# Retention in a two-block transformer kernel: a slab piece moved behind a head's outputs, ScalarE's copies moved ahead of SiLU, and one sum over added squares

## What is computed

```
def retention(q, k, v, g, positions):      # 4 heads; q, k: 128 wide, v, g: 256 wide
    q = rotary(q); k = rotary(k) * 128 ** -0.5
    scores = einsum('bnihd,bnjhd->bnhij', qc, kc) * decay_intra      # chunks of 128 tokens
    intra  = einsum('bnhij,bnjhe->bnihe', scores, vc)
    kv     = einsum('bnjhd,hj,bnjhe->nbhde', kc, decay_k, vc)
    _, prev = lax.scan(lambda state, kv_n: (decay_chunk * state + kv_n, state), 0, kv)
    cross  = einsum('bnihd,hi,nbhde->bnihe', qc, decay_q, prev)
    o = rms_norm(intra + cross)            # over the 256 features of one head
    return silu(g) * o                     # g = h @ w_in[:, 2048:3072]
```

## Time and profile before

| | us |
|---|---|
| median of 3 runs | 2892.36 |
| lowest and highest | 2891.91, 2897.39 |
| the profiled execution | 2891.22 |
| its span, first to last instruction | 2889.3 |
| TensorE busy | 2722.6 (94%) |
| VectorE busy | 1534.1 (53%) |
| ScalarE busy | 1106.3 (38%) |
| GpSimd busy | 906.2 (31%) |
| TensorE's granted clock, mean | 0.96 of full speed |

### The profile page before, as it was taken

The page is one execution under the profiler, slowest core; times in us unless marked ns, Lnnn a source line. Parts: engine busy times, 40 slices in busy tenths (PEclk is TensorE's granted clock), DMA queues, the critical chain, the costliest instruction groups (busy, mean ns, idle before and its releaser), DMA issues.

```text
span 2889.3 us, 34424 instructions
## 1 busy us (share of the span) xinstructions
PE 2722.6 (94%) x13278; PEld 2257.0 (78%) x13278; DVE 1534.1 (53%) x1676; ACT 1106.3 (38%) x1275; POOL 906.2 (31%) x200
## 2 busy tenths in 40 slices
PE   7899878999989999997989999899999979899997
PEld 5687567888769888886868888697988868788886
DVE  6755577699872420343256766754113351566666
ACT  3433353677642433334332233324432343332222
POOL 3211001000033244343434444242343433344343
PEclk9999698899999999998999999899999999999999
DMA  6110037499722122222234444221222222244443
GB/s 233 59 45 23 30 117 269 151 369 367 277 70 88 59 98 100 88 99 83 102 117 183 164 162 159 100 91 70 82 102 88 90 92 102 95 172 169 167 154 130
DMA packets 65320, 376.66 MB, mean 130 GB/s; under 512 B 7728, under 2 KB 8752, under 8 KB 29872
## 3 DMA queue, kind: packets, MB, share of 16 engines
q1 hardware_dynamic: 63040, 368.58, 35.1%
q10 hardware_dynamic: 2160, 6.42, 0.6%
HBM read 372.86 MB, written 2.10 MB: 130 GB/s over the span
## 4 chain that ended last, share of the span: by engine, by line
PE 75%; DVE 4%; issue 3%; POOL 1%; ACT 1%; ACTq 0%; DVEq 0%; POOLq 0%
PE pd L240 18%; PE pd L241 18%; PE pd L242 18%; PE pd L261 2%; PE pd L260 2%; PE pd L259 2%; PE pd L1768 2%; PE pd L1766 2%; PE pd L1767 2%; POOL sb_w_lo L218 1%; PE pd L1793 1%; DVE sb_ada_held L369 1%; PE pd L1795 1%; PE pd L1794 1%; PE pd L1724 1%
## 5 line engine op out<-in xcount | busy, mean ns | idle before, releaser
L218 POOL TENSOR_TENSOR sb_w_lo<-sb_raw,sb_w_hi 128x2048 fp32r<-128x2048 f32 x189 | 892.4, 4722 | 1792.7 <-ACT sb_w_hi L209 1792.7
L240 PE MATMUL pd<-sb_h_hi,sb_w_hi 128*128 128x512 f32 x1696 | 677.0, 399 | 44.0 <-DVE sb_h_lo L337 25.6
L241 PE MATMUL pd<-sb_h_lo,sb_w_hi 128*128 128x512 f32 x1696 | 666.7, 393 | 0.0
L242 PE MATMUL pd<-sb_h_hi,sb_w_lo 128*128 128x512 f32 x1696 | 666.0, 393 | 0.0
L209 ACT CAST sb_w_hi<-sb_raw 128x2048 fp32r<-128x2048 f32 x189 | 360.9, 1910 | 319.1 <-PE pd L242 315.0
L240 PEld LDWEIGHTS pd<-sb_h_hi,sb_w_hi 128*128 128x128 f32 x1696 | 322.8, 190 | 123.0 <-DVE sb_h_lo L337 29.7
L240 PE MATMUL pd<-sb_y_hi,sb_w_hi 128*128 128x512 f32 x960 | 377.2, 393 | 20.9 <-issue 17.0
L241 PE MATMUL pd<-sb_y_lo,sb_w_hi 128*128 128x512 f32 x960 | 376.4, 392 | 0.0
L242 PE MATMUL pd<-sb_y_hi,sb_w_lo 128*128 128x512 f32 x960 | 376.1, 392 | 0.0
L241 PEld LDWEIGHTS pd<-sb_h_lo,sb_w_hi 128*128 128x128 f32 x1696 | 322.8, 190 | 67.9 <-issue 2.2
L242 PEld LDWEIGHTS pd<-sb_h_hi,sb_w_lo 128*128 128x128 f32 x1696 | 322.3, 190 | 68.4
(11 more groups left out here) (502 smaller groups left out, 3918.1 us busy)
## 6 DMA issues: line engine op xcount, KB each, us to landing
sb_raw<-in_slabs SPq DMA_DIRECT2D x189, 1024.0 KB, 4.9
sb_V<-in_ada SPq DMA_DIRECT2D x64, 512.0 KB, 6.1
sb_V<-in_moe SPq DMA_DIRECT2D x28, 1024.0 KB, 7.1
sb_QK<-in_moe SPq DMA_DIRECT2D x28, 1024.0 KB, 7.1
sb_raw<-in_moe SPq DMA_DIRECT2D x28, 1024.0 KB, 6.8
sb_ada_held<-in_ada SPq DMA_DIRECT2D x36, 512.0 KB, 4.6
sb_QK<-in_ada SPq DMA_DIRECT2D x32, 512.0 KB, 6.7
sb_M<-in_ada SPq DMA_DIRECT2D x12, 512.0 KB, 14.3
```

The lines of the kernel that those rows point to most:

```text
L218: pool.tensor_tensor(w_lo[j][:], raw[j][:], w_hi[j][:].bitcast(F32), ALU.subtract).then_inc(w_lo_ready[j], 1)
L240: pe.matmul(out, w_hi[j][:, cols], hi[:, k], start=(k == 0), stop=False)
L241: pe.matmul(out, w_hi[j][:, cols], lo[:, k], start=False, stop=False)
L242: last = pe.matmul(out, w_lo[j][:, cols], hi[:, k], start=False, stop=(k == KT - 1))
```

## The change

Four things change, all in the retention loops.

- TensorE: `head_norm(h - 1)` moves from ahead of the gate slab to behind its third piece. The state products follow five pieces, not six. Of the remaining three pieces two stand ahead of the outputs, and the last one behind them.
- ScalarE: the wait for `ret_out` and the two copies stand ahead of SiLU instead of behind it. The squares stay behind SiLU.
- VectorE: `head_norm` begins with the sum of the two tiles of squares, behind both `ret_sq` signals, and signals `ret_added`.
- TensorE: `head_norm` has one matmul over that sum instead of two over the squares.

```diff
 # tensor engine
                 def head_norm(h):
-                    for et in range(2):
-                        pe.wait_ge(ret_sq, 8 * l + 2 * h + et + 1)
-                        last = pe.matmul(px[2][:], ones[:], T[:, et], start=(et == 0), stop=(et == 1))
-                    last.then_inc(ret_sum, 1)
+                    pe.wait_ge(ret_added, 4 * l + h + 1)
+                    pe.matmul(px[2][:], ones[:], T[:, 0], start=True, stop=True).then_inc(ret_sum, 1)
...
                     last.then_inc(ret_sc, 1)
+                    slab_starts(pe, L + L_G + h // 2, h % 2)
+                    for piece in range(3):
+                        slab_piece(pe, h % 2, piece, h_hi, h_lo)
                     if h:
                         head_norm(h - 1)
-                    slab_starts(pe, L + L_G + h // 2, h % 2)
-                    for piece in range(6):
+                    for piece in range(3, 5):
                         slab_piece(pe, h % 2, piece, h_hi, h_lo)
...
-                    for piece in range(6, KT):
+                    for piece in range(5, 7):
                         slab_piece(pe, h % 2, piece, h_hi, h_lo)
                     pe.wait_ge(ret_state, 4 * l + h + 1)
...
                     last.then_inc(ret_out, 1)
+                    slab_piece(pe, h % 2, KT - 1, h_hi, h_lo)
 # scalar engine
                     if h:
                         head_norm(h - 1)
+                    act.wait_ge(ret_out, 4 * l + h + 1)
+                    for et in range(2):
+                        act.copy(O[:, 2 * h + et], px[et][:]).then_inc(ret_stored, 1)
                     act.wait_ge(slab_done[j], m + 1)
                     act.wait_ge(ret_scaled, 4 * l + h + 1)
                     for f in range(2):
                         ins = act.activation(QK[:, 4 * f + h], pd[2 * j + f][:], ACT.Silu)
                     ins.then_inc(slab_out[j], 1)
-                    act.wait_ge(ret_out, 4 * l + h + 1)
-                    for et in range(2):
-                        act.copy(O[:, 2 * h + et], px[et][:]).then_inc(ret_stored, 1)
 # vector engine
                 def head_norm(h):

+                    dve.wait_ge(ret_sq, 8 * l + 2 * h + 2)
+                    dve.tensor_tensor(T[:, 0], T[:, 0], T[:, 1], ALU.add).then_inc(ret_added, 1)
                     dve.wait_ge(ret_root, 4 * l + h + 1)
```

More of the change, by code:

```diff
@@ L1518, in build @@
             "swapped", "rotated", "ret_sc", "ret_scaled", "ret_kv", "ret_state", "ret_out", "ret_stored"))
-        ret_sq, ret_sum, ret_root = (sem(n) for n in ("ret_sq", "ret_sum", "ret_root"))
+        ret_sq, ret_added, ret_sum, ret_root = (sem(n) for n in ("ret_sq", "ret_added", "ret_sum", "ret_root"))
         sgu_loaded, vs_root, vs_norm, sgu_w, mixed, mixed_out = (sem(n) for n in (
```

## The result

| | before | changed |
|---|---|---|
| median, us | 2896.12 | 2900.45 |
| lowest and highest, 11 runs each | 2891.78, 2900.58 | 2899.29, 2908.68 |
| ratio to before, 95% interval | | 1.0021 (1.0011 to 1.0031) |
| profiled execution: span, mean clock | 2889.3, 0.960 | 2901.9, 0.957 |

The change makes the kernel slower by 0.21%, 6 us (3 to 9 by the interval). Forecast were +11.9 us, twice as much; 2900.45 lies inside the range of 2894.5 to 2908. The kernel before had a median of 2896.12 in these runs, 3.7 us above the 2892.4 from which the forecast was counted, so the difference says more than the absolute time.

The account below looks back on a forecast made before the run. VectorE's serial chain, with 1.14 us to spare, was taken to become the bound through a later root; 3.6 us for waits plus 5 x 1.65 for clock falls gave +11.9, so 2892.4 + 11.9 = 2904.3 us, range 2894.5 to 2908.

Parts of the forecast that it names:

- VectorE's chain has 1.1 to 1.7 us to spare, and the change uses up 2.4 to 2.5: Retention heads: the root starts 2.4 to 2.5 us later, more than VectorE's serial chain to the state sums can spare.
- held about equally by both ways: Root's start at 7.7 us behind the outputs' end, set alike by ScalarE's order and by the sum's place on TensorE.
- The new wait of some 2.9 us: TensorE ahead of the outputs: there at 14.3, it waits some 2.9 us for VectorE's state sums; period 20.7.
- +3.6 us for the waits alone: Retention stage, both layers: +1.8 us per layer, +3.6 in all, from the new periods without falls of the clock.
- The table load costs 1.28 and no drain: ScalarE: each change of activation table costs 1.28 us, without the 1380 ns of draining the skill page gives.
- Rival 4: ScalarE: each table change also drains, 1.38 us more for each of two loads; +20 us, 2912 at least; chance 0.02.
- Five falls of the clock: TensorE's clock falls after five of six new waits, 1.65 us each, +8.3 us; four to six falls had chance 0.58.
- second case: New wait with two or three falls of TensorE's clock: +6.9 to +8.6 us, 2899 to 2901; chance 0.12.
- Slower by more than 0.2%: Whole kernel slower by more than the 0.2%, 5.8 us, that a measurement can tell; chance 0.74.
- within 0.2%: Whole kernel's time changes by no more than the measurable 0.2%, 5.8 us; chance 0.18.
- What moves without a price: ScalarE's next-slab cast comes 2.4 us later, with GpSimd's remainder; claimed free, cover 1.8 us at the last head.

Follow-up runs that it names:

- e5: Changed kernel with squares ahead of SiLU, VectorE's addition ahead of the score products, and the sum behind the first slab piece; ratio to before 1.0021.
- e9: Kernel before with the sum edit alone, the addition of squares on VectorE moved ahead of the score products; ratio to before 1.0028.
- e4_fill: Changed kernel plus nine matmuls per head (heads 1 to 3) into an unread bank, ahead of the wait for the states; ratio to before 1.0000.
- e1: Kernel before with only the sum edit: squares added on VectorE, summed by one matmul behind the third slab piece; ratio to before 1.0066.
- e6: As e5, with the root of heads 0 to 2 ahead of SiLU and the next slab's cast on ScalarE; ratio to before 1.0085.
- e7: As e6, with VectorE's running states also ahead of the remainders; ratio to before 1.0028.
- e8: As e7, with ScalarE's cast of the next slab ahead of the root; ratio to before 0.9961, median 2881.5 us.
- e2: Changed kernel without its sum edit: two sums directly behind the scores, no VectorE addition; ratio to before 1.0019.
- e3: Changed kernel with VectorE's running states ahead of the remainders of the norm; ratio to before 0.9973.
- e10: As e6, with the next slab's cast ahead of the root, running states still behind the remainders; ratio to before 0.9964.

## Why the prediction was right, and where it was not

- **VectorE's chain has 1.1 to 1.7 us to spare, and the change uses up 2.4 to 2.5.** Right. Forecast and measured, behind the outputs' end of the second period: scores 1.20 and 1.22, sum 6.65 and 6.70, root 7.7 and 7.76, reciprocal 8.4 and 8.39, states' end 17.2 and 17.15, outputs' start 17.3 and 17.20, period 20.7 and 20.59 to 20.70. e5 and e9 show separately that ScalarE's order and the sum's place each hold the root there, which the prediction put as "held about equally by both ways".
- **The new wait of some 2.9 us.** It is 2.67 to 2.76, since TensorE arrives at 14.5 and not at 14.3: the 4.03 for state products and two pieces was counted to the start of the next instruction, and the last matmul runs on for 0.2.
- **+3.6 us for the waits alone.** Right: +3.5 in e4_fill, where the clock holds.
- **The table load costs 1.28 and no drain.** Right: in the changed kernel SiLU starts 0.01 us behind its load, and the load 0.03 behind the copies. Rival 4 is out.
- **Five falls of the clock.** Here the forecast was too high: the profiled execution shows three, at 1.6 us each. The price of a fall (1.65) was right, the count was not. I had carried it over from waits of 2.8 us and more, which all had ended with a fallen clock (behind the wait for the first load there are 14 of them in the trace, not 12, and the clock is 0.50 to 0.54 behind each), while the new waits are of 2.67 to 2.76; both of 2.67 us left the clock alone and three of the four of 2.76 did not. Three falls are the prediction's own second case ("two or three falls", +6.9 to +8.6), in which the stage's +8.3 lies, and not its likeliest. That the median too falls between the 2899 and 2901 of that case is partly luck, since the kernel before was 3.7 us slower in these runs than the forecast's base. In the ratio, 6 us less the 3.6 leave 2.5 us or 1.5 falls on average, with an interval from none to three.
- **Slower by more than 0.2%.** The ratio's middle is 0.21% and its interval begins at 0.11%, so the sign is measured and the size stands on that bound. The direction for which 0.74 was given is right; a case for "within 0.2%" was worth more than 0.18.
- **What moves without a price.** Right in the changed kernel, but by luck: the argument looked only at when the slab is wanted, and not at what GpSimd's shifted operation runs beside. There it runs from 966.77 to 971.34, beside VectorE's wait for the root and the reciprocal. The addition of two SBUF tiles had ended 1.1 us ahead of it, and the next operation on two SBUF tiles starts 0.8 us behind it. In e1, e6 and e7 the two met, and that was the largest effect of the study.

## What to carry to other kernels

Filling a wait is worth nothing if the step that fills it pushes back the start of a serial chain on another engine: before moving work, write down for each engine the chain between the two points of synchronisation and its margin, here 1.1 us on VectorE. Ahead of a wait of TensorE put first what TensorE waits for, and leave operations that only later stages need (here the remainders) behind it. And when one engine's operation moves, look at what it now lies beside, not only at when its result is wanted.

## What the runs showed of the hardware

**VectorE and GpSimd exclude each other for some operations.** A VectorE operation on two tiles, both in SBUF, took 0.69 us alone and 4.96 us when GpSimd's subtraction of two SBUF tiles (4.56 us) had begun 0.15 us ahead of it; a pair of such operations took 5.46 instead of 1.29. Moving only the order, e9 and e8 had 0.69 and 1.29 again. It goes the other way too: in e6, where VectorE's product was in work when GpSimd's operation started, the latter took 4.95 instead of 4.6. An addition with one input in a PSUM bank kept its 0.69 us (kernel before, at 165.06, beside GpSimd's operation of 162.44 to 167.20), and so did the reciprocal its 3.35 us in e8, where it starts at 940.77 beside a subtraction that lasts to 943.42. But one SBUF input alone does not make an operation safe: in the kernel before, a TENSOR_SCALAR on one SBUF tile takes 0.43 us at 828.98 and 4.83 us beside GpSimd:

```profile
829.42 4.57 POOL L218 TENSOR_TENSOR sb_w_lo<-sb_raw,sb_w_hi 128x2048 fp32r<-128x2048 f32 x1 [16.23 <-ACT sb_w_hi L209]
```
```profile
829.44 4.83 DVE L2399 TENSOR_SCALAR sb_MG<-sb_MG 128x512 f32<-128x512 f32 x1
```

The collision on two tiles also stands in the trace of the kernel before, just ahead of the wait at 847.63 that the prediction reads in the earlier trace rows:

```profile
842.89 4.68 POOL L218 TENSOR_TENSOR sb_w_lo<-sb_raw,sb_w_hi 128x2048 fp32r<-128x2048 f32 x1 [8.90 <-ACT sb_w_hi L209]
```
```profile
843.20 4.93 DVE L2413 TENSOR_TENSOR sb_QK<-sb_QK,sb_T 128x512 f32<-128x512 f32 x1
```

So the miss in e1 could have been foreseen from rows. The Trainium skill, "SBUF — State Buffer", section "Who interferes with whom", says that a VectorE instruction with two SBUF inputs contends with a GpSimd instruction that reads SBUF and that whoever comes first holds the shared ports for its whole instruction; the rows here on two SBUF inputs agree. I had not put this rule to the change.

**TensorE's clock.** In the heads of these kernels, waits of 2.31 to 2.33 us (e1, all six heads), of 2.73 to 2.79 (11 of 14 in the changed kernel, e5 and e7), and of 4.27 and more (e6, all six) were followed by a clock below 1.00; the four of 2.63 to 2.67 (changed kernel and e5), waits of up to 1.5 us (e2, e3, e9, e10) and of 0.7 (e4) never were. A fall cost 1.6 us in the changed kernel, and idle time that is filled with useless matmuls kept it away. So the length of a wait does not tell by itself whether the clock falls: why those of 2.63 to 2.67 left it alone, and those of 2.31 in e1 did not, is open; e1 has two more short waits in each period.
